# Compact GLA scores, joined row statistics and folded sample maps in a two-layer encoder step

## What is computed

```python
o_a, s_gla = _gla_chunked(q_a, k_a, v_a, log_a, s_gla0)     # 4 heads, dk 32, dv 64, decay per token and channel
o_a = _rms_norm(o_a, P['gla_norm'][l]) * jax.nn.silu(gr)
o_d = _diff_attention(q_d, k_all, v_all, pos, arange, lam)  # 4 heads, dv 128; softmax map 0 - lam * softmax map 1
o_d = _rms_norm(o_d, P['diff_subln'][l]) * (1.0 - lam_init)
o_r, s_ret = _retention_chunked(q_r, k_r, v_r, s_ret0)      # 4 heads, dk 64, dv 64
o_r = _layer_norm(o_r, P['ret_norm'][l]) * jax.nn.silu(rg)
out = concat([o_a, o_d, o_r]) @ P['w_out'][l]
```

## Time and profile before

| | |
|---|---|
| runs | 1412.16 us median of 3 (1411.04 to 1413.54) |
| profiled execution | 1408.09 us, span from first to last instruction 1406.3 us |
| granted TensorE clock, mean | 0.992 of 2.4 GHz |
| PE busy | 1362.9 us, 97% of the span |
| DVE, ACT, POOL busy | 57%, 44%, 9% |
| mixer of layer 0, of layer 1 (input projection up to the fourth step of the output projection) | from 274.2 to 439.4 us, from 965.1 to 1128.9 us |

### The profile page before, as it was taken

One profiled execution on the slowest core, in us unless ns is written; L12 is line 12 of the kernel. 1 busy time (PEld: TensorE's weight loads), 2 busy tenths in 40 slices (PEclk: granted clock), 3 DMA queues, 4 the chain that ended last, 5 costly groups with the idle time before them and its releaser, 6 DMA issues.

```text
span 1406.3 us, 24734 instructions
## 1 busy us (share of the span) xinstructions
PE 1362.9 (97%) x9649; PEld 1326.6 (94%) x9649; DVE 807.3 (57%) x1224; ACT 625.0 (44%) x987; POOL 130.4 (9%) x129
## 2 busy tenths in 40 slices
PE   6999999989999999999999999999899999999998
PEld 6999999978899999999999999999788999999998
DVE  4655544687655665564366555347865467555542
ACT  4444444552344554443454444346324455444333
POOL 2000000360000200000020000013500011000000
PEclk9999999999999999999999999999999999999999
DMA  5755555442233355545545554564322344555552
GB/s 154 204 165 164 161 159 155 139 108 77 79 113 102 103 155 149 149 142 149 153 116 149 148 150 147 148 175 112 86 78 84 98 120 123 149 149 149 149 145 72
DMA packets 351770, 187.34 MB, mean 133 GB/s; under 512 B 6316, under 2 KB 348600, under 8 KB 351704
## 3 DMA queue, kind: packets, MB, share of 16 engines
q1 hardware_dynamic: 348368, 177.49, 44.8%
q0 software_dynamic: 2496, 7.93, 1.6%
q10 hardware_dynamic: 840, 0.99, 0.3%
HBM read 182.07 MB, written 4.33 MB: 133 GB/s over the span
## 4 chain that ended last, share of the span: by engine, by line
PE 86%; DVE 6%; DMA 3%; ACT 2%; issue 1%; DVEq 1%; POOL 1%; ACTq 0%; SPq 0%; POOLq 0%
PE ps L616 26%; PE ps L617 26%; PE ps L618 26%; DVE w_l L495 2%; DVE scores L1423 1%; PE ps L905 1%; DMA raw<-in_w_in_dram 1%; PE ps L915 1%; DMA raw<-in_ffn_w_up_dram 1%; PE ps L804 1%; PE ps L926 1%; PE ps L672 1%; PE ps L679 1%; PE ps L879 1%; DMA raw<-in_w_out_dram 0%
## 5 line engine op out<-in xcount | busy, mean ns | idle before, releaser
L616 PE MATMUL ps<-xn_l,w_h 128*128 128x320 f32 x1840 | 579.9, 315 | 3.0 <-DVE xn_l L1260 2.0
L618 PE MATMUL ps<-xn_h,w_h 128*128 128x320 f32 x1840 | 569.2, 309 | 0.0
L617 PE MATMUL ps<-xn_h,w_l 128*128 128x320 f32 x1840 | 569.0, 309 | 0.0
L495 DVE TENSOR_TENSOR w_l<-raw,w_h 128x1024 fp32r<-128x1024 f32 (+1 forms) x340 | 408.3, 1203 | 181.9 <-ACT w_h L486 181.8
L486 ACT ACTIVATE w_h<-raw 128x1024 fp32r<-128x1024 f32 (+1 forms) x342 | 353.2, 1035 | 262.8 <-DMA raw<-in_ffn_w_down_dram 130.0
L616 PEld LDWEIGHTS ps<-xn_l,w_h 128*128 128x128 f32 x1840 | 346.4, 188 | 12.8 <-issue 3.6
L617 PEld LDWEIGHTS ps<-xn_h,w_l 128*128 128x128 f32 x1840 | 346.6, 188 | 0.7
L618 PEld LDWEIGHTS ps<-xn_h,w_h 128*128 128x128 f32 x1840 | 346.4, 188 | 0.0
L616 PE MATMUL ps<-hid_l,w_h 128*128 128x320 f32 x704 | 217.4, 309 | 0.0
L617 PE MATMUL ps<-hid_h,w_l 128*128 128x320 f32 x704 | 217.3, 309 | 0.0
L618 PE MATMUL ps<-hid_h,w_h 128*128 128x320 f32 x704 | 217.3, 309 | 0.0
(11 more groups left out here) (226 smaller groups left out, 1182.6 us busy)
## 6 DMA issues: line engine op xcount, KB each, us to landing
raw<-in_ffn_w_up_dram SPq DMA_DIRECT2D x176, 512.0 KB, 3.9
raw<-in_ffn_w_down_dram SPq DMA_DIRECT2D x64, 448.0 KB, 3.8
raw<-in_w_in_dram SPq DMA_DIRECT2D x54, 512.0 KB, 3.8
raw<-in_ffn_w_down_dram SPq DMA_DIRECT2D x32, 512.0 KB, 4.0
raw<-in_w_out_dram SPq DMA_DIRECT2D x16, 512.0 KB, 4.0
const<-in_tables_dram POOLq DMA_DIRECT2D x8, 272.0 KB, 4.4
x_in<-in_x_prompt_dram SPq DMA_DIRECT2D x1, 1024.0 KB, 3.8
scores<-in_cache_diff_k_dram POOLq DMA_DIRECT2D x2, 512.0 KB, 5.1
```

The lines of the kernel that those rows point to most:

```text
L495: dve.tensor_tensor(w_l[s][:, 0:cols], raw[s][:, 0:cols], w_h[s][:, 0:cols], ALU.subtract).then_inc(w_lo, 1)
L616: pe.matmul(out, w_h[s][:, w], xl, start=first, stop=False)
L617: pe.matmul(out, w_l[s][:, w], xh, start=False, stop=False)
L618: return pe.matmul(out, w_h[s][:, w], xh, start=False, stop=last)
```

## The change

1. **GLA levels, compact.** Levels 2 to 8 need only the two diagonal 64x64 pieces of each block. They are now made as 64x64 matmuls, the lower half of a block into partitions 0 to 63 and the upper into 64 to 127: 24 matmuls in level 2, 20 in each of the levels 3 to 8, where there were 12. Level 1 has 8 matmuls as before, but of 64x64. DVE's masked copy is over 3 x 64 columns per head instead of 3 x 128, into `near`, which lies in the buffer of `probs` and is zeroed by one more POOL memset. After level 8 ACT copies `near` into `scores` in three operations (`placed`), and `gla_o` waits for that.
2. **Sample maps folded.** For b 2 `att_t` multiplies the probabilities with a 128x64 matrix `fold` that adds the two maps, instead of transposing them. ACT then copies 64 columns instead of 128, and `att_o` takes each key tile once.
3. **Statistics.** For the tiles 0, 1, 2, 3, 6 and 7 one matmul each (weights `mean`, 44 columns wide, moving side the squares, 320 columns) accumulates all row sums in bank 3 as [44, 320]. Root and reciprocal work on 44x320; DVE splits the result into a rounded part and a rest (`inv_2`), and `spread` is one matmul of fp32r with `pick`. Tiles 4 and 5 keep the old form, each with its own `stat`.
4. **Order.** `root` is a step of its own, apart from `stat`. `squares a` moves from after `att_o 8` to after `tok 3`, `stat a` from after `att_o 9` to before `att_t 8`, `root a` to just behind `att_s 10`, `att_a 9`. `HEAD_ORDER` is (2, 3, 4, 5, 0, 1, 6, 7): the last attention head goes fourth instead of last. The level steps stand one half tile later, `gla_keys` further behind; `tok 0` goes before `att_s 0`, `tok 5` before `att_s 5`, `ret_state` before `att_t 0`.
5. The masks come in one DMA, `pick` in another, both on POOL's queue in layer 0 during the first feed-forward block.

The diff, cut to its core:

```diff
-HEAD_ORDER = (2, 3, 4, 0, 1, 6, 7, 5)
-STAT_HEADS = {"a": (0, 1, 6, 7, 2, 3, 4), "b": (5,)}
+ROW_AT = {0: (0, 2), 1: (2, 2), 6: (4, 2), 7: (6, 2), 2: (8, 1), 3: (9, 1)}
+HEAD_ORDER = (2, 3, 4, 5, 0, 1, 6, 7)
+STAT_OF = {"b": 4, "c": 5}
...
-    + [("level", 0), ("part", 8, 0, 5), ("weight", 2), ("level", 1), ("part", 8, 5, 8), ("part", 9, 0, 2), ("weight", 3), ("level", 2),
+    + [("part", 8, 0, 5), ("weight", 2), ("level", 0), ("part", 8, 5, 8), ("part", 9, 0, 2), ("weight", 3), ("level", 1),
...
-    + [("att_t", 9), ("att_s", 11), ("att_a", 10)] + P8[26][:1] + [("att_o", 9), ("stat", "a")] + P8[26][1:]
+    + [("stat", "a"), ("att_t", 8), ("att_s", 10), ("att_a", 9), ("root", "a")] + P8[25][:1] + [("att_o", 8)] + P8[25][1:]
+    + [("att_t", 9), ("att_s", 11), ("att_a", 10)] + P8[26][:1]
+    + [("att_o", 9), ("squares", "b"), ("att_a", 11), ("spread", 2), ("spread", 3), ("lo", 2), ("lo", 3)] + P8[26][1:]
...
-        if c:
-            m = (r[:, None] // (2 * c) == r[None, :] // (2 * c)) & (r[:, None] % (2 * c) < c) & (r[None, :] % (2 * c) >= c)
+    for c in LEVELS[2:]:
+        t = 64 * half[:, None] + np.arange(64)[None, :]
@@ POOL, past 1
+                        pool.memset(near[:, :, :], 0.0)
                         pool.memset(scores[:, :, :, :], 0.0).then_inc(mem_set, 1)
@@ PE, level
-                    todo = [(3, 0, 1)] if n == 0 else [(0, 1, 1), (2, 0, 0)] if n == 1 else [(0, 1, 1), (1, 2, 2), (2, 0, 0)]
+                    todo = [(tile, at, b) for at, tile in ((0, 1), (1, 2), (2, 0)) for b in range(2) if n == 2 or (at, b) != (1, 0)]
...
+                                out, k, q = ps_m[64 * b:64 * b + 64, h, 64 * at:64 * at + 64], slice(s0, s0 + 64), slice(t0, t0 + 64)
+                            mm = pe.matmul(out, ks[r, k], qs[r, q], start=True, stop=True, skip_group_check=True)
@@ PE, gla_o
-                    after(pe, l, "dve", "score8")
+                    after(pe, l, "act", "placed")
@@ PE, att_t
+                            mm = pe.matmul(ps[:, 6, kt * P:kt * P + T_S], p, C("fold"), start=True, stop=True)
@@ PE, stat
+                            mm = pe.matmul(bank3[0:44, 0:T], C("mean")[:, 44 * q:44 * q + 44], z[:, q, :], start=q == rows[0],
@@ PE, spread (j-th of HEAD_ORDER; it waits for head j - 2, the first two for att_max11)
+                    if n in ROW_AT:
+                        mm = pe.matmul(ps[:, bank, 0:T], pick[0:44, n, :], inv_2[0:44, :], start=True, stop=True)
@@ ACT, level 8
+                        for b in (0, 2):
+                            act.activation(scores[0:64, :, b, 0:64], from_near[0:64, :, b, :], ACT.Copy)
+                        mark("act", act.activation(scores[64:P, :, 0:3, 64:P], from_near[64:P, :, :, :], ACT.Copy), "placed")
@@ ACT, root
+                    dst, src = (root_a, bank3[0:44, 0:T]) if n == "a" else (var_h[:, STAT_OF[n] - 4, :], ps[:, STAT_BANK[n], T:T + 3])
@@ DVE, level
-                            i = dve.copy_predicated(flat[:, :, a:b], m, ps_m[:, :, a:b])
+                        i = dve.copy_predicated(near, mask[:, n - 2:n - 1, :].broadcast_to([P, H, 3 * 64]), ps_m[:, :, 0:3 * 64])
@@ DVE, root
+                    if n == "a":
+                        dve.reciprocal(inv_a, root_a)
+                        dve.drain()
+                        dve.tensor_copy(inv_2[0:44, :], inv_a)
+                        dve.drain()
+                        i = dve.tensor_tensor(inv_2[32:44, :], inv_a[32:44, :], inv_2[32:44, :], ALU.subtract)
```

More of the change, by code:

```diff
@@ L88 @@
+    + [("tok", 0), ("att_s", 0)] + P8[15][:1] + [("tok", 4)] + P8[15][1:]
     + [("att_s", 1), ("att_a", 0), ("ret_s", 1)] + P8[16]
-    + [("att_t", 0), ("att_s", 2), ("att_a", 1), ("ret_state",)] + P8[17][:1] + [("att_o", 0), ("ret_o", 0)] + P8[17][1:]
+    + [("ret_state",), ("att_t", 0), ("att_s", 2), ("att_a", 1)] + P8[17][:1] + [("att_o", 0), ("ret_o", 0)] + P8[17][1:]
     + [("att_t", 1), ("att_s", 3), ("att_a", 2), ("ret_o", 1)] + P8[18][:1] + [("att_o", 1), ("ret_mu", 0)] + P8[18][1:]
@@ new lines @@
+    + [("att_t", 9), ("att_s", 11), ("att_a", 10)] + P8[26][:1]
+    + [("att_o", 9), ("squares", "b"), ("att_a", 11), ("spread", 2), ("spread", 3), ("lo", 2), ("lo", 3)] + P8[26][1:]
+    + [("att_t", 10), ("stat", "b"), ("att_o", 10), ("att_t", 11), ("root", "b"), ("out", 0), ("att_o", 11), ("squares", "c"),
+       ("spread", 4), ("stat", "c"), ("root", "c"), ("lo", 4), ("gates",), ("out", 1), ("spread", 5), ("spread", 0), ("lo", 5),
+       ("out", 2), ("lo", 0), ("spread", 1), ("spread", 6), ("lo", 1), ("out", 3), ("spread", 7), ("lo", 6), ("lo", 7), ("ahead",),
+       ("out", 4), ("out", 5), ("out", 6), ("out", 7)]
@@ L231, in constants @@
     add("bias", np.concatenate([bias(r, r), bias(128 + r, np.arange(256)), b2], axis=1))
[L232 to L239 removed]
+    mean, pick = np.zeros((P, 8, 44)), np.zeros((P, 8, P))
+    for q, (c, w) in ROW_AT.items():
+        for h in range(w):
+            rows = slice(h * P // w, (h + 1) * P // w)
+            for g in (0, 32):
+                mean[rows, q, g + c + h] = w / P
+                pick[g + c + h, q, rows] = 1.0
+    add("mean", mean.reshape(P, -1))
+    add("fold", r[:, None] % T_S == np.arange(T_S)[None, :])
+    add("pick", pick.reshape(P, -1))
+    masks, half = [], r // 64
+    for c in LEVELS[2:]:
+        t = 64 * half[:, None] + np.arange(64)[None, :]
+        s = r[:, None]
+        m = (s // (2 * c) == t // (2 * c)) & (s % (2 * c) < c) & (t % (2 * c) >= c) if c else s == t
+        masks.append(np.concatenate([m, m & (half[:, None] == 1), m], axis=1))
     return np.concatenate(parts, axis=1), at, np.concatenate(masks, axis=1).astype(np.uint8)
```

142 lines of the change are left out of this document (76 added, 66 removed).

## The result

The changed kernel takes 1393.88 us (median of 4, 1392.57 to 1394.79), the kernel before beside it 1411.87 (median of 4, 1411.04 to 1413.54): ratio 0.9887, 95% interval 0.9867 to 0.9906, so 13 to 19 us less. Forecast were 1397.5 us, 14.6 less than before.

The account below looks back on a forecast made before the run. PE, busy 97% of the span, was taken as the bound, with DVE almost setting the level stage's pace. Terms of -0.8, -2.1, -0.9 and -3.5 us a layer took the profiled 1408.1 to 1393.5, so 1397.5 as median; range 1386 to 1411.

Parts of the forecast that it names:

- Levels, waits: Level stage: PE's waits on DVE's scores, `z`, `q_s` and POOL go, 4.3 us a layer.
- Levels, matmuls: Level stage: more small matmul records, at 0.030 us each, add 3.5 us of PE time a layer.
- the row of L760: Four profiled records of the 32x64 shape, 0.33 us for all, one taking 0.24: read as 0.030 us apart.
- The lower bound of 0.0145: Level matmuls: spacing in us a record if only streamed columns counted, half of 0.029.
- The rule that the text set beside it: Level matmuls: 8 independent 32x64 tiles where 32x128 has 4, so a level step of 0.81 us.
- columns only: Rival, level matmuls: 64x64 tiles overlap fully, a step costs 0.81 us, -4.3 a layer, 1389 us; chance 0.15.
- Levels together: Level stage: waits -4.3 and matmuls +3.5 make -0.8 us a layer.
- Order and folded maps: Moved `tok 0`, `tok 5`, `ret_state`: -2.1 us a layer; sample maps folded, two heads ahead of the end stage: -0.9.
- End: End stage: 32.5 us instead of 36.05, -3.5 a layer, with 27.2 of PE work and 5.0 of new waits.
- I add 0.3 for an even chance that the clock falls: End stage: allowance in us for the clock falling in the spread wait, 1.4 for twelve products, mostly inside ACT's lateness.
- the end gives more back: Rival, end stage: DVE and ACT wait on each other, clock falls, +3 us a layer, 1403.5 us; chance 0.13.
- The sum: Whole kernel: levels -0.8, order -2.1, folded maps -0.9, end -3.5 make -7.3 us a layer, -14.6 in all.

Follow-up runs that it names:

- experiment 2: Changed kernel with rotations 2 and 3 moved later, behind level 5 and behind `tok 11`: 1389.47 us, ratio 0.9863 to the kernel before.
- experiment 8: Changed kernel with statistic a's root ahead of map 10's softmax maximum and rotations 2 and 3 earlier, behind levels 0 and 1: 1375.9 us, ratio 0.9762.
- experiment 1: Changed kernel with each small matmul of levels 3 to 8 issued twice: 1403.66 us, ratio 0.9963 to the kernel before.
- the change once more: Changed kernel run again unchanged, beside the later experiments: 1392.99 us, ratio 0.9881 to the kernel before.
- experiment 4: Changed kernel with the sample maps as before (transposes, both map halves, longer copies): 1389.49 us, ratio 0.9862 to the kernel before.
- experiment 11: Kernel of experiment 8 with map 10's transposes two product groups before tile 26's end and `tok 9` behind tile 7: 1373.18 us, ratio 0.9724.
- experiment 10: Kernel of experiment 8 with the sample maps as before (transposes, twice as many matmuls): 1379.40 us, ratio 0.9773 to the kernel before.
- experiment 12: Kernel of experiment 11 with `tok 9` moved once more, into the block of level 2: 1381.86 us, ratio 0.9799 to the kernel before.
- experiment 7: Kernel before with only `tok 0`, `tok 5` and `ret_state` in the places the change gives them: 1403.89 us, ratio 0.9958.
- experiment 9: Changed kernel with six idle 128x256 matmuls issued in the wait ahead of the first new spread: 1390.64 us, ratio 0.9844.
- experiment 3: Changed kernel with statistic a's root right behind its matmuls, ahead of map 10's softmax maximum: 1385.55 us, ratio 0.9823.
- experiment 6: Kernel before with the compact levels and their order alone: 1406.15 us, ratio 0.9976 to the kernel before.

## Why the prediction was right, and where not

**Levels, waits: wrong by half.** "I expect the waits ... to go: 4.3 us." 2.3 and 2.8 us remained, at level 3, `tok 10` and level 4. The masked copies are 1033 ns as priced, and DVE has 5 to 6 us less work in the stage (39.92 to 33.99). But an average says nothing of the place: between levels 1 and 4 DVE has, in each of two steps, a rotation's three operations, a masked copy, a `z` and a `w_l`: 5.4 us of them from 303.8 to 309.2, while PE's step from level 2 to level 3 has 3.8 of work. Experiments 2 and 8 show it: moved later the rotations took 2.4 us of waits along, moved earlier they left 0.5.

**Levels, matmuls: wrong in sign.** The term +3.5 (0.030 us a record) is about -1.5: a step costs PE 0.73 us from start to start where it cost 0.97 (each less the product's own 0.147), over six levels. The step that failed is the choice of the row of L760: four records cannot tell a spacing from what the first one takes. The lower bound of 0.0145 was right within the measured 0.013 (0.71 for 40, one taking 0.22) to 0.018 (experiment 1). The rule that the text set beside it, 8 tiles of 32x64 (the Trainium skill, TensorEngine Tiling (Array Packing), Available Configurations), and which it laid aside on the word of L760, gives 0.81 us a step; 0.71 was measured, so on this point the trace agrees with the rule. So the rival *columns only* came true in its price. Two further steps got cheaper that the sum had at nothing or dearer: level 1, whose 8 matmuls now have 64 columns each, by 0.27 us, and level 2 by 0.17 in place of +0.70. Levels together: -3.8 a layer in place of -0.8. From start to start all small steps of the stage take 4.3 us less in either layer (20.7 and 21.0 before, 16.4 and 16.6 after): 2.2 to 2.4 of waits, with those on `gv_tok` and behind level 8 counted in, and 1.9 of the level steps. In layer 0 the fallen clock takes back 1.1 on the products.

**Order and folded maps: right together (-3.0 forecast, -2.97 measured), off apart.** Order alone gives -2.5 (-2.1 forecast), the fold in this stage -0.4 (-0.9 forecast): 0.38 a head against 0.43, but head 0's is eaten by a wait at `tok 1` that the text had not seen.

**End: its waits near, the clock wrong, PE's own work too short.** The wait at the spread is 3.0 (3.2 forecast), the reciprocal 2.15 (2.15), the copy of `att_t 10` 1.0 in layer 0 (1.3), `stat c` 0.4 (0.5): 4.4 together where the sum had 5.0. Up to behind the fourth step of the output projection the end takes 34.65 and 36.30 us, not 32.5. What failed first is "I add 0.3 for an even chance that the clock falls". In the four traces with the full 3.0 us wait (the change, the change once more, experiments 1 and 2) the clock is under 1.00 in every end stage, 8 of 8; in the change it cost 1.6 us in layer 0 and 3.2 in layer 1. That is the distance from the 32.5 us that the same stage (up to the last spread) takes in experiment 4, whose clock did not fall. The second failure is smaller: PE's own small steps are 14.4 us, not 13.0 (in layer 0 34.65 us, less 0.15 of the product that opens the window, 14.1 of the other products, 4.4 of waits and 1.6 of clock; the trace of experiment 11 gives 14.4 as well). The six new spreads alone take some 2.0 from start to start where the text had nearly 1. Clock, own work and shorter waits together make the 3 a layer of the rival *the end gives more back*; of its mechanism the fall of the clock came true, while the waits of DVE and ACT on each other were in the forecast already.

**The sum.** Levels came out 3.0 a layer below their term and the end 3.0 above its own, so that the forecast was met because two errors cancelled. The number was luck: its working was wrong in two of four terms. Nor did the levels' term miss as one rival alone would: the matmuls' price was off by 5, and the waits that stayed took some 2 of it back.

## What to carry to other kernels

A wait that goes with a step is found by following the step: ask for each engine what it has to do between the two events, not how busy it is over the stage, and ask it again for the place to which a step is moved, on the shared bank above all. A milestone belongs on the operation that last reads what is waited for, not on the last of its step. What PE saves is only saved where the next release is already there; the fold was worth nothing until the root had been moved. Price a series from a long series: where only four records exist, keep both bounds open in the sum.

## What the runs showed of the hardware

- Float32 matmuls of 32 rows and 64 columns on 64x64 output tiles follow each other 0.013 to 0.018 us apart in series of 40 to 80 records.
- The clock, level stages. With the compact levels and the waits at `tok 10` and level 4 it was under 1.00 in 10 of 14; with them gone or spread (experiments 2, 8, 10, 11) in 0 of 8; with 2.6 us at `tok 9` (experiment 12) in 1 of 2; in the old form, whose waits of 0.6 to 1.45 us stand apart, in 0 of 4 (the kernel before, experiment 7).
- The clock, end stages, by the place of the fall. At the 3.0 us wait it fell in 7 of 8 stages, from 1.5 us before the wait's end to 0.3 behind it; with 2.33 us (experiment 4) in 0 of 2, filled (9) in 0 of 2, with none (3, 8, 10, 11, 12) in 0 of 10. Behind the small matmuls with the 0.9 to 1.04 us wait for ACT it fell in three: layer 0 of the change and of experiment 9, layer 1 of experiment 3. A standstill is not needed: in the old form (the kernel before, experiments 6 and 7), where PE works through 42 records of one or two columns without a wait, it fell in these or within 1 us behind them in 6 of 6. Against the same stage at a clock of 1.00 a fall behind the wait for ACT cost 1.6 us (0.94 or 0.95 over the stage); a fall at the 3.0 us wait cost 3.0 to 3.4 where the stage had 0.86, but 0.4 where it had 0.95 (layer 0 of experiment 1, layer 1 of experiment 2), since with PE slowed the wait for ACT was gone. So wait and clock together were worth 4.7 to 6.4 us where the wait itself was 3.0 (the end stages of the change against those of experiment 8). That the wait as such is the cause is likely by these counts and not shown: whatever removed it also moved the work around it.
- DVE operations with two inputs in SBUF are stretched by POOL's, and POOL's by DVE's: in layer 0 L1522 takes 0.48 to 1.37 us and L1524 0.49 to 1.69, while L1521 beside them, with one input in PSUM, stays at 0.49. DVE's timeline after, rotation 2:

```profile
303.80 0.49 DVE L1521 TENSOR_TENSOR y<-ps,const 128x320 f32<-128x320 f32 x1 [1.39 <-PE ps L856]
304.20 1.37 DVE L1522 TENSOR_TENSOR z<-z,const 128x320 f32<-128x320 f32 x1
305.65 0.85 DVE L1524 TENSOR_TENSOR z<-z,y 128x320 f32<-128x320 f32 x1
```

  The Trainium skill (GPSIMD Engine Reference, Specifications, the row on SBUF interfaces) says that POOL contends with DVE instructions that have two SBUF inputs; the trace agrees. It also shows the size: the one that starts second ends some 0.35 us behind the first, if it is of 320 elements. POOL's L548 ran from 303.67 to 305.23 and L1522 ended at 305.57; its L539 ended at 306.15 and L1524 at 306.50; its L548 at 311.62 and the next L1524 at 311.97. Where DVE was first, POOL was the longer: L548 at 309.77 takes 1.85 us, while L1522, begun at 309.73, has its 0.48. So the stretch is about what is left of the other's operation; in DVE's step from 303.8 to 309.2 it is 1.2 of 5.4 us. No run here took POOL's work away to test it.
- A reciprocal of 320 elements takes 2.15 us (L1559, 2145 ns); the line through the 0.18 us of 3 and the 0.36 of 33 elements had given 2.15. The estimate of 2.7 us from the repeat count of 8 (the Trainium skill, VectorE: DVE Perf Modes, Walkthrough: the 8-slice pipeline in each mode) was too long.
